# The modulation product of a two-block transformer kernel: raw fp32 weights on four column groups in place of rounded high and low halves

## The reference, cut to what matters

```python
c_act = jax.nn.silu(c)[:, None, :]
cc_act = jax.nn.silu(c_ctx)[None, None, :]
for i in range(DEPTH):                      # 2 layers
    mx = jnp.split(c_act @ ada_w[i] + ada_b[i], 6, axis=-1)
    mc = jnp.split(cc_act @ ada_w[i] + ada_b[i], 6, axis=-1)
    h_x = modulate(rms_norm(x, norm1_g[i]), mx[0], mx[1])
    h_c = modulate(rms_norm(y_ctx, norm1_g[i]), mc[0], mc[1])
    ...                                     # attention (layer 0) or retention (layer 1), then swiglu
```

## Time and profile before

| | us |
|---|---|
| three runs, median (lowest to highest) | 2746.81 (2741.6 to 2750.44) |
| the profiled execution, its own time | 2745.91 |
| its span from the first to the last instruction | 2744.0 |
| granted TensorE clock, mean share of full | 0.983 |
| PE busy | 2641.0 (96%), 18318 instructions |
| DVE busy | 1554.6 (57%) |
| ACT busy | 1298.4 (47%) |

### The profile page before, as it was taken

The page is one execution under the profiler, slowest core; times in us unless marked ns, Lnnn a source line. Parts: engine busy times, 40 slices in busy tenths (PEclk is TensorE's granted clock), DMA queues, the critical chain, the costliest instruction groups (busy, mean ns, idle before and its releaser), DMA issues.

```text
span 2744.0 us, 48185 instructions
## 1 busy us (share of the span) xinstructions
PE 2641.0 (96%) x18318; PEld 2364.6 (86%) x18318; DVE 1554.6 (57%) x2375; ACT 1298.4 (47%) x1931; POOL 130.3 (5%) x108
## 2 busy tenths in 40 slices
PE   5999998999998999999999999999999999999998
PEld 4746557888887997899999998899999999989998
DVE  4457774433325424565566665776656657567664
ACT  4447773322214333344444458654444445865543
POOL 3000000000000000000000001210000000211000
PEclk8979999999999999999999999999999999999999
DMA  7235552233233333345555555436556465544653
GB/s 251 70 99 178 180 159 85 92 100 99 86 96 106 96 93 129 100 150 181 183 179 169 173 181 155 148 124 179 180 177 184 154 196 154 173 130 138 184 179 120
DMA packets 398662, 398.39 MB, mean 145 GB/s; under 512 B 17360, under 2 KB 396768, under 8 KB 398544
## 3 DMA queue, kind: packets, MB, share of 16 engines
q1 hardware_dynamic: 395680, 390.25, 45.9%
q0 software_dynamic: 2864, 6.57, 0.8%
HBM read 395.72 MB, written 1.05 MB: 145 GB/s over the span
## 4 chain that ended last, share of the span: by engine, by line
PE 82%; DVE 7%; issue 4%; ACT 4%; DMA 1%; POOL 1%; SPq 0%; ACTq 0%; DVEq 0%; POOLq 0%
PE acc L747 64%; PE acc L732 4%; PE acc L804 3%; DVE w_lo L1633 2%; PE wk L871 2%; ACT w_hi L1116 1%; DMA raw<-in_ada_w_dram 1%; PE wk L894 1%; PE acc L894 1%; PE wk L813 1%; PE wk L823 1%; PE wk L956 1%; DVE h_lo L1736 1%; PE acc L997 1%; PE wk L997 1%
## 5 line engine op out<-in xcount | busy, mean ns | idle before, releaser
L1633 DVE TENSOR_TENSOR w_lo<-raw,w_hi 128x1024 fp32r<-128x1024 f32 x752 | 927.2, 1248 | 769.2 <-ACT w_hi L1116 761.5
L747 PE MATMUL acc<-h_hi,w_hi 128*128 128x256 f32 (+1 forms) x3696 | 1110.0, 300 | 26.3 <-DVE h_lo L1736 8.5
L747 PE MATMUL acc<-h_lo,w_hi 128*128 128x256 f32 (+1 forms) x3696 | 1105.8, 299 | 0.0
L747 PE MATMUL acc<-h_hi,w_lo 128*128 128x256 f32 (+1 forms) x3696 | 1105.5, 299 | 0.0
L1116 ACT CAST w_hi<-raw 128x1024 fp32r<-128x1024 f32 x752 | 764.8, 1032 | 495.1 <-PE acc L747 414.6
L747 PEld LDWEIGHTS acc<-h_hi,w_hi 128*128 128x128 f32 x3696 | 710.8, 192 | 51.2 <-issue 19.6
L747 PEld LDWEIGHTS acc<-h_hi,w_lo 128*128 128x128 f32 x3696 | 711.0, 192 | 20.9
L747 PEld LDWEIGHTS acc<-h_lo,w_hi 128*128 128x128 f32 x3696 | 711.1, 192 | 20.5
L747 PE MATMUL acc<-hid_hi,w_hi 128*128 128x256 f32 (+1 forms) x1056 | 317.6, 301 | 4.3 <-DVE w_lo L1633 4.3
L747 PE MATMUL acc<-hid_hi,w_lo 128*128 128x256 f32 (+1 forms) x1056 | 318.9, 302 | 0.0
L747 PE MATMUL acc<-hid_lo,w_hi 128*128 128x256 f32 (+1 forms) x1056 | 317.8, 301 | 0.0
(11 more groups left out here) (343 smaller groups left out, 2544.6 us busy)
## 6 DMA issues: line engine op xcount, KB each, us to landing
raw<-in_w_in_dram SPq DMA_DIRECT2D x100, 512.0 KB, 4.2
raw<-in_ada_w_dram SPq DMA_DIRECT2D x96, 512.0 KB, 3.9
raw<-in_ffn_w_in_dram SPq DMA_DIRECT2D x88, 512.0 KB, 3.5
raw<-in_ffn_w_gate_dram SPq DMA_DIRECT2D x88, 512.0 KB, 4.1
raw<-in_ffn_w_up_dram SPq DMA_DIRECT2D x88, 512.0 KB, 4.1
raw<-in_ffn_w_down_dram SPq DMA_DIRECT2D x80, 512.0 KB, 3.7
raw<-in_ret_w_qkvg_dram SPq DMA_DIRECT2D x48, 512.0 KB, 3.6
raw<-in_ffn_w_out_dram SPq DMA_DIRECT2D x40, 512.0 KB, 3.5
```

The costliest lines, as they stand in the source:

```text
L747: mm = pe.matmul(o, ws[:, s, k, c], xs[:, kk, t], start=(u == 0 and k == 0 and i == 0), stop=(last and k == nk - 1 and i == 2))
L1633: dve.tensor_tensor(w_lo[:, s, 0:nk, :], raw[:, s, 0:nk, :], w_hi[:, s, 0:nk, :], ALU.subtract).then_inc(lo_done, 1)
```

## The change

The modulation product no longer uses split weights. PE multiplies the raw fp32 unit as soon as its load has landed; ACT and DVE do nothing with the unit. The two vectors stand as fp32 in `c_wide`, 8 chunks of 32 stationary columns of which the first 2 hold c and c_ctx and 30 are zero; it lies in `nomask`, which DVE sets back to zero after the last unit of `ada1` (semaphore `c_zero`). The four chunks of a unit go to four column groups of the array, 32 columns and 32 output partitions each, so the accumulator holds four partial sums on partitions 0-1, 32-33, 64-65 and 96-97; the copy to `ada_s` and the product with `sel` take 128 partitions, and `sel` adds the four. A slot of `raw` that held a modulation unit is refilled when PE has used it (`units_used`), and the split counters skip those units (`split0`). On DVE the copy of the inputs stands between the second and third block pair of ada0a.

```diff
-        "sel": np.repeat(np.eye(2), 2, axis=0)[np.minimum(p, 3)] * (p < 4)[:, None],
+        "sel": np.stack([p % 32 == w for w in range(2)], axis=1),
...
-        c_parts = sb("c_parts", [P, DC, 4], F32R)
+        c_wide = nomask[:].rearrange("p (k m) -> p k m", m=32)
...
# SP, stream():
-                        sp.wait_ge(lo_done, job.unit(l, it, p) + 1)
+                        held = after if p < SLOTS else name
+                        if held in ADA:
+                            sp.wait_ge(units_used, job.unit(l, it, p) + 1)
+                        elif held and name in ADA:
+                            sp.wait_ge(lo_done, J[held].split(l, J[held].iters - 1, J[held].body - SLOTS + p) + SLOTS + 1)
+                        elif held:
+                            sp.wait_ge(lo_done, job.split(l, it, p) + 1)
...
# PE, modulation_unit():
-                unit_ready(job, None, it, p)
+                pe.wait_ge(load[p % SLOTS], job.loaded(None, it, p))
                 for k in range(KCH):
-                    for i, ws in enumerate((w_hi, w_lo)):
-                        mm = pe.matmul(acc[0:4, b % 2, 0, 0:S], c_parts[:, u * KCH + k, :], ws[:, p % SLOTS, k, :],
-                                       start=(u == 0 and k == 0 and i == 0), stop=(u == 1 and k == KCH - 1 and i == 1))
+                    mm = pe.matmul(acc[32 * k:32 * k + 32, b % 2, 0, 0:S], c_wide[:, u * KCH + k, :], raw[:, p % SLOTS, k, :],
+                                   start=(u == 0), stop=(u == 1), tile_position=(0, 32 * k), skip_group_check=True)
                 mm.then_inc(units_used, 1)
...
-                return pe.matmul(dst, ada_s[0:4, c * P:(c + 1) * P], sel[0:4, :], start=True, stop=True)
+                return pe.matmul(dst, ada_s[:, c * P:(c + 1) * P], sel[:, :], start=True, stop=True)
...
# ACT, beside_first(): no splits; the copy is 128 partitions wide
-                for k in range(SIDE_UNITS):
-                    if side_step(k) == i:
-                        name, it, p = side_unit(k)
-                        split(J[name], None, it, p)
...
-            head("ada0a")
-            rest("ada0a", None)
             squares(0, 0, (x_done, 4))
             squares(1, 1, (x_done, X_START))
-            head("q0", None, "ada0a", None)
+            head("q0")
...
# DVE
-            head("ada0a")
-            rest("ada0a", ada, None, [lambda: None, inputs])
-            head("q0", None, "ada0a", ada)
+            ada(0)
+            ada(1)
+            inputs()
+            for it in range(2, J["ada0a"].iters):
+                ada(it)
+            head("q0")
...
             dve.wait_ge(pt_ok, ITEMS0)
+            dve.wait_ge(units_used, J["ada1"].unit(None, J["ada1"].iters - 1, J["ada1"].body - 1) + SLOTS + 1)
+            dve.memset(nomask[:], 0.0).then_inc(c_zero, 1)
```

More of the change, by code:

```diff
@@ L111, in unit, with split @@
         return self.unit0 + p + it * self.body + (l * self.unit_step if self.unit_step else 0)
+    def split(self, l, it, p):
+        return self.unit(l, it, p) - self.unit0 + self.split0
     def block(self, l, it, b):
@@ L168, with unsplit_before, job_before @@
 JOBS = plan()
+ADA = ("ada0a", "ada0b", "ada1")
+def unsplit_before(name):
+    return sum(J.iters * J.body for n, J in JOBS.items() if n in ADA and J.unit0 < JOBS[name].unit0)
+for name in JOBS:
+    JOBS[name].split0 = JOBS[name].unit0 - unsplit_before(name)
+def job_before(name):
+    order = FIRST + SECOND
+    return order[order.index(name) - 1] if name != order[0] else None
 NORMS1 = 7
@@ L375, in build @@
         turned = sem("turned")
-        c_ok, c_hi_ok, c_lo_ok = sem("c_ok"), sem("c_hi_ok"), sem("c_lo_ok")
+        c_ok, c_zero, c_wide_ok = sem("c_ok"), sem("c_zero"), sem("c_wide_ok")
         soft_a, soft_v = sem("soft_a"), sem("soft_v")
@@ L506, in stream, with one @@
                 job = J[name]
-                def one(it):
+                def one(it, after=name):
                     for p in range(job.body):
-                        sp.wait_ge(lo_done, job.unit(l, it, p) + 1)
+                        held = after if p < SLOTS else name
[5 more added lines that the diff above has]
+                            sp.wait_ge(lo_done, job.split(l, it, p) + 1)
                         s = src(l, it, p)
@@ L516, in one @@
                         sp.dma_start(dst, s).then_inc(load[p % SLOTS], 16)
+                before = job_before(name)
                 if job.iters == 1:
                     one(0)
+                elif before is None or (before in ADA) != (name in ADA):
+                    one(0, before)
+                    with sp.Fori(1, job.iters) as it:
+                        one(it)
                 else:
@@ L699, in unit_ready @@
             def unit_ready(job, l, it, p):
-                pe.wait_ge(lo_done, job.unit(l, it, p) + SLOTS + 1)
+                pe.wait_ge(lo_done, job.split(l, it, p) + SLOTS + 1)
             def slot_free(job, l, it, b):
@@ L1263, in attention @@
                             .then_inc(p_ok, 1)
+                        if again:
+                            act.wait_ge(c_zero, 1)
                         if G["sink"] is not None:
@@ L1304, in beside_first @@
                         c += 16 if name == "ada0b" else 0
-                        act.copy(ada_s[0:4, c * P:(c + 2) * P], acc[0:4, p // 2 % 2, 0, 0:S]).then_inc(acc_free, 1)
+                        act.copy(ada_s[:, c * P:(c + 2) * P], acc[:, p // 2 % 2, 0, 0:S]).then_inc(acc_free, 1)
             def squared(name):
@@ L1433, in _ @@
             act.wait_ge(c_ok, 1)
-            cc = c_act[:].rearrange("p (w k) -> p k w", w=2)
-            act.copy(c_parts[:].rearrange("p k (w s) -> p k w s", s=2)[:, :, :, 0], cc).then_inc(c_hi_ok, 1)
-            head("ada0a")
-            rest("ada0a", None)
+            act.copy(c_wide[:, :, 0:2], c_act[:].rearrange("p (w k) -> p k w", w=2)).then_inc(c_wide_ok, 1)
             squares(0, 0, (x_done, 4))
             squares(1, 1, (x_done, X_START))
-            head("q0", None, "ada0a", None)
+            head("q0")
             pair_deviations(0, 0)
@@ L1631, in split @@
                 s, nk = p % SLOTS, job.unit_chunks[p]
-                dve.wait_ge(hi_done, job.unit(l, it, p) + 1)
+                dve.wait_ge(hi_done, job.split(l, it, p) + 1)
                 dve.tensor_tensor(w_lo[:, s, 0:nk, :], raw[:, s, 0:nk, :], w_hi[:, s, 0:nk, :], ALU.subtract).then_inc(lo_done, 1)
@@ L1637, in split_diag @@
                 hi, lo = [w_diag[:, p - 2, n].rearrange("p (c j) -> p c j", j=P) for n in range(2)]
-                dve.wait_ge(hi_done, job.unit(l, 0, p) + 1)
+                dve.wait_ge(hi_done, job.split(l, 0, p) + 1)
                 dve.tensor_tensor(lo[0:64, :, 0:64], src[0:64], hi[0:64, :, 0:64], ALU.subtract)
@@ L1764, in attention @@
                         if again:
+                            dve.wait_ge(c_zero, 1)
                             dve.memset(passed[:, c:c + 1], 0.0)
@@ L1795, in attention, with ada @@
                         beside(i)
[L1797 to L1806, removed]
+            def ada(it):
+                for b in range(J["ada0a"].per):
+                    block_done(J["ada0a"], None, it, b)
+                    at = (it * J["ada0a"].per + b) * COLS
+                    dve.tensor_copy(ada_s[:, at:at + COLS], acc[:, b, 0, 0:S]).then_inc(acc_free, 1)
             def residual(layer, gate, both, bpi):
@@ L2015, in _ @@
                     dve.tensor_tensor(qk[:, n, 0:S], rot_b[:, b % 2, 0, :], rot_b[:, b % 2, 1, :], ALU.add).then_inc(hqk, 1)
-                beside_first(c - 11)
-            attention("first", groups_first(), None, beside_first)
+            attention("first", groups_first(), None)
             head("wo0")
             dve.wait_ge(pt_ok, ITEMS0)
+            dve.wait_ge(units_used, J["ada1"].unit(None, J["ada1"].iters - 1, J["ada1"].body - 1) + SLOTS + 1)
+            dve.memset(nomask[:], 0.0).then_inc(c_zero, 1)
             modulations(2, 0, mod[:, 0, 16:48, :], 16, 48)
```

8 lines of the change are left out of this document (2 added, 6 removed).

## The result

The changed kernel takes 2715.06 us (median of 4 runs, 2711.7 to 2721.49) against 2745.35 us for the kernel before: ratio 0.9891, 95% interval 0.9866 to 0.9916. It is 30 us faster where 18 us slower was forecast. Its profiled execution took 2721.49 us, 24.4 us less than the one of before.

The account below looks back on a forecast made before the run. PE was taken to bound the attention, so PE's cost per modulation unit decides. From 2745.9 us, +21 (attention), +3 (lower clock), 0 (187 to 201 us) and -6 (start) give +18: 2764 us, range 2705 to 2800.

Parts of the forecast that it names:

- The bound: Attention, 201 to 405 us: PE busy 204.00 of 204.00 us, so taking work from ACT and DVE buys nothing there.
- The price of one instruction: Modulation unit on PE: 0.215 us per fp32 instruction of 256 columns, plus 0.15 us for going into and out of a group.
- the three forms: Cost of a modulation unit on PE: 1.87 us one after the other, 0.58 all groups at once, 1.01 a further case.
- The step that failed: Modulation unit on PE: instructions start in program order, 1.22 us, 0.30 more than now; +21 us over the attention's 70 units.
- The rule on weight loads: Modulation units: a page rule would expose eight more weight loads in each unit; the forecast left them out of the sum.
- Half clock, units: Five side units at the lower clock, 157 to 187 us: 2.3 us each against 1.71, +3 us.
- 187 to 201 us: Stretch before the attention, DVE full, five units: about -1.7 + 1.5 us, taken as 0.
- The start: 0 to 60 us: PE uses units without waiting for splits and slots are refilled earlier, -6 us.
- rival D: About 1.01 us a unit, or the clock before the attention rises earlier: 2737 to 2752 us, chance 16%.
- a sign of being wrong: Attention: the prediction is wrong if PE shows gaps there or the clock there falls below 1.00.
- Rival B: All four column groups run at once, 0.58 us a unit: -37 us, 2709 us, chance 30%.
- the rivals' chances: Whole kernel against the one before: faster 34%, same 13%, slower 53%.

Follow-up runs that it names:

- e7: Changed kernel, with ACT casting and DVE subtracting a resident tile for each of the 80 side units, result unread: 2713.43 us.
- e1: Changed kernel with all four chunks of a unit accumulated on column group 0, no column groups: 2807.52 us, ratio 1.0243 to the kernel before.
- e12: Kernel before, with one unused full-height 128x256 matmul after each of the nine side units before the attention: 2742.05 us.
- e8: Changed kernel with one unused 128-row, 256-column fp32 matmul after each of the nine side units before the attention: 2704.8 us.
- e3: Changed kernel on two column groups, chunks 0 and 1 on the first, 2 and 3 on the second: 2741.47 us.
- e14: Changed kernel with unused matmuls: four in PE's gap before the rotation, one after each of three headback products and nine side units: 2701.35 us.
- e10: Changed kernel with one unused matmul of only 20 rows after each of the nine side units before the attention: 2733.52 us.
- e13: Changed kernel with unused matmuls: four in the gap before the rotation, one after each of three headback products and the first four side units: 2709.47 us.
- e2: Changed kernel on two column groups, chunk k on group k mod 2: 2737.47 us, ratio 0.9984 to the kernel before.
- e5: Changed kernel with four unused fp32 matmuls in PE's 4.21 us wait for the reciprocal before the rotation: 2718.89 us.

## Why the prediction was wrong

- **The bound** was right. PE is full in the attention, ACT and DVE are not: e7 puts their work back at 0.6 us, and e1 shows that the change with their relief and without the column groups would lose 63 us.
- **The price of one instruction** was right: 0.215 us for 256 columns of fp32 and about 0.15 us around a group. From it the three forms follow to 0.03 us (1.87, 1.01 and 0.58 expected, 1.84, 1.00 and 0.57 measured).
- **The step that failed** is the sentence "I take 1.22 us ... because the engine has one queue and the trace gives only starts in the order of the program". A waiting second instruction of a pair holds nothing back. Instead of 70 x 0.30 = +21 us the stretch had 70 x -0.35 = -24 us by its units; at full clock it measured -25.3 (e12 against e8). No row of before had two column groups, and the choice between 0.58 and 1.22 rested on none; that the trace shows starts in order where every instruction needs the whole array is no evidence for instructions that don't. The Trainium skill, "TensorE: Matmul & The Clock Gate", was used for two things. That starts on different tiles are some 4 ns apart, in section "Measured speedup vs the span model", agrees with the unit of 0.57 us, though the starts measured here are 7 ns apart. That starts and ends keep program order stands in its section "The mechanism", not where the prediction puts it; the staggering that I derived from it does not agree (e3, 1.00 instead of 1.65 us), and neither do e3's starts.
- **The rule on weight loads**, from the Trainium skill, same page, section "The mechanism", would have exposed eight loads of 0.11 us a unit. The trace disagrees: in e1, with all rows and one group in use, a unit of 1.84 us is 8 x 0.215 and 0.12, with no room for them. Leaving it out was right.
- **Half clock, units**: +3 us was forecast for five units. A unit at half clock takes 1.01 instead of 1.71 us, so that term too has the other sign.
- **187 to 201 us**: taken as 0, and from the start of the rotation to the first scores 0.5 us was gained. That it came out is luck: faster units, no wait on DVE and a longer half clock cancelled. At nearly equal clock the rotation became 3.0 us shorter (e12 against e8).
- **The start**: -6 us forecast, -8.5 measured. The mechanism was right, its size too small. PE's transposes started at 26.87 instead of 33.61, where 30.8 was expected, since the loads of the first units had waited on the splits as well; the turned chunks came 1.01 us after the start of the last unit, as summed (1.2).
- **The clock** was seen only as a possible gain (rival D). It fell in the changed kernel for 65 instead of 31 us, and below 1.00 in the attention, which the prediction itself names as a sign of being wrong. Rival B's sum of -37 us was right for the change itself (e12 against e8: 37.3), its terms less so: 25.3, 3.0 and 8.6 us where it has 24, 7 and 6. But 30 came out. The longer half clock took the rest: the attention took 201.8 us in the changed kernel's profile and 191.0 to 191.3 in e8 and e14.
- **Small slips** that change nothing: an fp32 instruction costs 1.9 times the fp32r one (0.215 against 0.115 us), not twice; all at once, five units at half clock give 5 x -0.65 = -3.3 us, not -4; and the rivals' chances add up to 34% faster, 12% same and 54% slower.

Open is why the profile of e10 held the half clock longer even than the changed kernel, and how much of e13's spread (2700.66 to 2713.25) comes from the place at which its clock fell, since one profile shows one such place. The longer half clock itself is in all four runs of the changed kernel. That it comes from the change's thinner stream fits e1, e2 and e8 to e14, but it was not isolated: no run thins the stream of the kernel before, and what exactly starts the fall at 150 us is not shown.

## What to carry to other kernels

Where a product has few rows, plain fp32 on four column groups costs 2 x 0.215 + 0.15 us for four chunks of 256 columns, less than the split form with its eight fp32r matmuls, and needs neither casts nor remainders; count the instructions of the fullest group; the three orders tried here made no difference. Ask of every piece of work that is made shorter or thinner on TensorE what the clock does next: look at the granted clock by stretch, not at the mean, and if a thin, PE-bound stretch runs at half clock, try a few full-height matmuls without use in it. Compare at equal clock before judging a change of 1%.

## What the runs showed of the hardware

- Matmuls of different column groups run beside each other even if an earlier one of another group is still waiting: 8, 4 and 2 instructions on the fullest group give 1.84, 1.00 and 0.57 us, and four on four groups start some 7 ns apart.
- The clock fell to half in the middle of back-to-back products of 20 rows and partner products (e5, at 154 us, PE busy 5.42 of the 6 us before), and came back 3 us after the first fill of 128 rows (e8, at 164 us), but not with fills of 20 rows (e10, 75 us at half clock).
- TensorE work without use can pay: nine matmuls of 128x256 made the changed kernel 10 us faster, sixteen placed through the thin stretch 14 us.
